# A column-chunk projection whose opening is widened from three chunks to seven, with shift products in column groups

## The reference

```
mod = silu(c) @ w_ada + b_ada                 # 2048 x 6144
shift, scale, gate = split(mod, 3)
h = rms_norm(x, norm_g) * (1 + scale) + shift
proj = h @ w_in                               # 2048 x 13824, parts u, zp, q, kv, za, a, b, zc, gates
y_pool = pooling(u) * silu(zp); y_attn = attention(q, kv) * silu(za)
y_conv = conformer(a * sigmoid(b)) * silu(zc) # depthwise width 31, layer norm, pointwise
merged = sum over branches of sigmoid(gate_i) * (y_i @ w_branch_i)
out = rms_norm(x + gate * (merged @ w_out), final_g)
```

## Time and profile before

| what | value |
|---|---|
| median of three runs | 1021.48 us (1018.66 to 1022.21) |
| profiled execution, time | 1021.49 us |
| profiled execution, span | 1019.7 us |
| TensorE busy | 971.0 us (95%) |
| VectorE busy | 673.6 us (66%) |
| ScalarE busy | 411.3 us (40%) |
| transfers | 220 MB, 216 GB/s on the mean |

### The profile page before, as it was taken

How to read it: one execution, slowest core, us unless ns; L and a number is a source line. 1 busy time by engine, 2 the same in 40 slices (tenths; PEclk the granted TensorE clock), 3 DMA queues, 4 the chain that set the end, 5 groups by cost and what they waited for, 6 DMA issues and landing times.

```text
span 1019.7 us, 10210 instructions
## 1 busy us (share of the span) xinstructions
PE 971.0 (95%) x4227; PEld 755.6 (74%) x4227; DVE 673.6 (66%) x775; ACT 411.3 (40%) x363; POOL 9.8 (1%) x27
## 2 busy tenths in 40 slices
PE   4879999999999999999998999999999999999996
PEld 1124567888888888888887777888888888887885
DVE  3656674767858877876765644368657889766463
ACT  4131244343344334344355434435643333444432
POOL 2000000000000000000000000000000000000000
PEclk9889999999999999999998987999999999999999
DMA  9899997565555565665553343355468998975512
GB/s 313 310 332 366 342 370 240 166 205 166 166 165 187 186 205 179 197 203 184 188 165 124 110 137 125 116 173 199 145 234 315 391 341 300 323 250 182 186 62 82
DMA packets 107758, 220.00 MB, mean 216 GB/s; under 512 B 3665, under 2 KB 3745, under 8 KB 106945
## 3 DMA queue, kind: packets, MB, share of 16 engines
q1 hardware_dynamic: 106304, 212.88, 61.2%
q0 software_dynamic: 1120, 5.43, 1.5%
q10 hardware_dynamic: 288, 1.05, 0.3%
HBM read 217.25 MB, written 2.10 MB: 215 GB/s over the span
## 4 chain that ended last, share of the span: by engine, by line
PE 83%; DVE 6%; DMA 4%; ACT 4%; issue 2%; SPq 0%; DVEq 0%; ACTq 0%
PE acc_odd L941 12%; PE acc_even L941 12%; PE acc_odd L942 12%; PE acc_odd L943 12%; PE acc_even L942 12%; PE acc_even L943 12%; DMA raw<-in_w_ada 4%; PE side_b L969 4%; ACT wh L378 2%; DVE wl L584 2%; DVE ada_sums L631 1%; PE side_a L1052 1%; ACT probs L425 1%; PE side_b L955 1%; PE side_a L955 1%
## 5 line engine op out<-in xcount | busy, mean ns | idle before, releaser
L584 DVE TENSOR_TENSOR wl<-raw,wh 128x2048 fp32r<-128x2048 f32 x152 | 347.7, 2291 | 274.5 <-ACT wh L378 274.2
L378 ACT ACTIVATE wh<-raw 128x2048 fp32r<-128x2048 f32 x152 | 290.7, 1913 | 324.1 <-PE acc_even L943 144.8
L941 PE MATMUL acc_even<-wh,act_h 128*128 128x512 f32 x480 | 192.3, 401 | 1.8 <-DVE glu_a L821 0.9
L941 PE MATMUL acc_odd<-wh,act_h 128*128 128x512 f32 x480 | 189.5, 395 | 1.5 <-DVE wl L584 1.5
L943 PE MATMUL acc_even<-wh,act_l 128*128 128x512 f32 x480 | 188.7, 393 | 0.0
L942 PE MATMUL acc_even<-wl,act_h 128*128 128x512 f32 x480 | 188.5, 393 | 0.0
L943 PE MATMUL acc_odd<-wh,act_l 128*128 128x512 f32 x480 | 187.5, 391 | 0.0
L942 PE MATMUL acc_odd<-wl,act_h 128*128 128x512 f32 x480 | 187.4, 390 | 0.0
L941 PEld LDWEIGHTS acc_even<-wh,act_h 128*128 128x128 f32 x480 | 91.3, 190 | 22.9 <-issue 1.7
L941 PEld LDWEIGHTS acc_odd<-wh,act_h 128*128 128x128 f32 x480 | 90.5, 189 | 23.2 <-issue 2.7
L943 PEld LDWEIGHTS acc_even<-wh,act_l 128*128 128x128 f32 x480 | 91.1, 190 | 19.5
(11 more groups left out here) (239 smaller groups left out, 762.7 us busy)
## 6 DMA issues: line engine op xcount, KB each, us to landing
raw<-in_w_in SPq DMA_DIRECT2D x108, 1024.0 KB, 5.1
raw<-in_w_ada SPq DMA_DIRECT2D x48, 1024.0 KB, 7.0
raw<-in_w_out SPq DMA_DIRECT2D x16, 1024.0 KB, 5.0
raw<-in_w_branch_pool SPq DMA_DIRECT2D x8, 1024.0 KB, 5.0
raw<-in_w_branch_attn SPq DMA_DIRECT2D x8, 1024.0 KB, 4.9
raw<-in_w_branch_conv SPq DMA_DIRECT2D x8, 1024.0 KB, 6.1
raw<-in_conv_pw SPq DMA_DIRECT2D x4, 1024.0 KB, 5.3
x_tok<-in_x SPq DMA_DIRECT2D x1, 2048.0 KB, 8.3
```

The source lines that it names most:

```text
L378: nc.scalar.activation(wh[:, m % RING], raw[:, g % RING], ACT.Copy).then_inc(high_done, 1)
L584: nc.vector.tensor_tensor(wl[:, m % RING], raw[:, load_of(m) % RING], wh[:, m % RING].bitcast(F32), ALU.subtract).then_inc(raw_done, 1)
L941: nc.tensor.matmul(sums[:, h, :], xh, wh[:, slot, i, :], start=begin, stop=False)
```

## The change

Seven chunks are open at once: a0, b0, a1, b1, u0, u1, zp0. Of each K quarter all seven pieces are made before the next quarter: piece m = 7k + j is quarter k of chunk j. The first two chunks stay in the two accumulators. The five others (PARTS) have no room in PSUM: for each token half a quarter's product goes to one of three banks in turn (two of pa, one of pb, `halves`), and is copied to SBUF by ScalarE in quarter 0 (`keep`) or added to it by VectorE in quarters 1 and 2 (`add_part`). The last quarter, pieces 21 to 27, goes through the ordinary loop into accumulators, and VectorE adds the stored sum (`last_part`). ScalarE's evacuations of u0 and u1 go away; sigmoid of b1 and SiLU of zp0 work from SBUF.

The load order has all of the shift and scale loads of quarter k + 1 among the seven weights of quarter k. There are six raw buffers until the load of piece 21, four after.

A shift product has a stationary side of 32 equal columns (c_wide) at column group t for K tile t, so the four products of a shift piece write four different groups of 32 partitions of pb; they are picked and summed over partitions with one more product (`pick`). The scale sums are summed over partitions by products with a column of ones instead of transposes and a reduction. h is made by ScalarE alone (4 ACTIVATEs into h_tmp, one copy to act_h), VectorE makes act_l. VectorE sums scale load 0 before the norm of x. The pool_w load is issued after the transposes of x, no longer after h. Later steps (transposes, pool windows, pool mix, taps) are shifted to new steps; the taps go to steps 26 to 87, four each, instead of 13 to 79.

The loops over k in the diff are, in this order, those of ScalarE, of VectorE and of TensorE; the shift products stand ahead of `halves`.

```diff
+OPEN = ("a0", "b0", "a1", "b1", "u0", "u1", "zp0")
+QUARTERS = 4
+WIDTH = len(OPEN)
+OPENING = WIDTH * QUARTERS
+STAY = 2
+for _i in range(4):
+    LOADS += [("shift", 0, _i), ("scale", 0, _i)]
+for _k in range(QUARTERS):
+    for _j in range(WIDTH):
+        LOADS += [("weights", WIDTH * _k + _j, 0)]
+        if _k + 1 < QUARTERS and 2 <= _j < 6:
+            LOADS += [("shift", _k + 1, _j - 2), ("scale", _k + 1, _j - 2)]
...
+RAWS = 6
...
+    _s = _g % RAWS if _g <= LOAD_OF["weights", WIDTH * (QUARTERS - 1), 0] else min(range(RING), key=_last.get)
...
-TAPS_AT = {m: 4 if m < 22 else 2 if m < 32 else 4 for m in range(13, 80)}
+TAPS_AT = {m: 4 for m in range(26, 88)}
+QUAD = 32
...
+        part_banks = [pa[:, 0:COLS], pa[:, COLS:2 * COLS], pb[:, COLS:2 * COLS]]
+        def part_turn(m, h):
+            return 2 * (PARTS * (m // WIDTH) + m % WIDTH - STAY) + h
...
-            pool.wait_ge(h_ready, 4)
-            pool.wait_ge(consts_ready, 1)
+            pool.wait_ge(x_t, 4)
             pool.dma_start(pool_w[:, :, :, :], a["pool_w"][0].rearrange("g (k p) n -> p g k n", p=P)
                            ).then_inc(pool_w_loaded, 16)
+            pool.wait_ge(h_ready, 4)
...
+            def modulate(q):
+                act.wait_ge(mod_ready, q + 1)
                 if q:
+                    act.wait_ge(h_ready, q)
                 for t in range(PK):
+                    last = nc.scalar.activation(h_tmp[:, t, :], x_chan[:, PK * q + t, :], ACT.Identity,
                                                 scale=mod_scale[:, t:t + 1], bias=mod_shift[:, t:t + 1])
+                last.then_inc(h_full, 1)
+                act.wait_ge(h_full, q + 1)
+                nc.scalar.activation(act_h[:, PK * q:PK * q + PK, :], h_tmp[:, :, :], ACT.Copy).then_inc(h_high, 1)
+            def keep(m):
+                act.wait_ge(used, m + 1)
+                for h in range(TH):
+                    nc.scalar.activation(part[CHUNK_OF[m][0]][:, h, :], part_banks[part_turn(m, h) % 3], ACT.Copy
+                                         ).then_inc(part_copied, 1)
+            for k in range(QUARTERS - 1):
+                m = WIDTH * k
+                split(m + 1)
+                split(m + 2)
+                if k == 1:
+                    keep(m - 1)
+                split(m + 3)
+                split(m + 4)
+                if k == 0:
+                    keep(m + 2)
+                    keep(m + 3)
+                split(m + 5)
+                if k == 0:
+                    keep(m + 4)
+                copy_shift(k + 1)
+                split(m + 6)
+                if k == 0:
+                    keep(m + 5)
+                split(m + 7)
+                modulate(k + 1)
...
+            def last_part(name):
+                total = part[name][:, :, :]
+                dve.wait_ge(used, END[name])
+                dve.wait_ge(part_added, 4 * PARTS)
+                ins = nc.vector.tensor_tensor(total, sums_of(name)[:, :, :], total, ALU.add)
...
+            for k in range(QUARTERS - 1):
+                m = WIDTH * k
+                split(m + 1)
+                split(m + 2)
+                if k == 2:
+                    add_part(m - 1)
+                scale_piece(k + 1, 0)
+                split(m + 3)
+                scale_piece(k + 1, 1)
+                if k:
+                    add_part(m + 2)
+                split(m + 4)
+                scale_piece(k + 1, 2)
+                if k:
+                    add_part(m + 3)
+                split(m + 5)
+                if k:
+                    add_part(m + 4)
+                scale_piece(k + 1, 3)
+                split(m + 6)
+                if k:
+                    add_part(m + 5)
+                modulation_columns(k + 1)
+                split(m + 7)
+                hidden_low(k + 1)
...
                 for t in range(PK):
-                    k = PK * i + t
-                    ins = nc.tensor.matmul(pb[0:1, 0:COLS], c_act[:, k:k + 1], raw[:, g % RING, t, :],
-                                           start=(k == 0), stop=(k == KT - 1))
+                    rows = slice(QUAD * t, QUAD * (t + 1))
+                    ins = nc.tensor.matmul(pb[rows, 0:COLS], c_wide[:, PK * i + t, :], raw[SLOT_OF[g]][:, t, :],
+                                           start=(i == 0), stop=(i == 3), tile_position=(0, QUAD * t))
...
+            def halves(m):
+                pe.wait_ge(raw_done, raws(load_of(m)))
+                for h in range(TH):
+                    turn = part_turn(m, h)
+                    if 3 <= turn < 3 + 2 * PARTS:
+                        pe.wait_ge(part_copied, turn - 2)
+                    elif turn >= 3:
+                        pe.wait_ge(part_added, turn - 2 - 2 * PARTS)
+                    for i in range(PK):
+                        ins = products(act_h, act_l, PK * (m // WIDTH) + i, m % RING, i, part_banks[turn % 3], h,
+                                       i == 0, i == PK - 1)
+                ins.then_inc(used, 1)
...
+            for k in range(QUARTERS - 1):
+                pe.wait_ge(h_ready, k + 1)
+                for j in range(WIDTH):
+                    m = WIDTH * k + j
+                    if j < STAY:
+                        piece(act_h, act_l, PK * k, m, sums_of(OPEN[j]), k == 0, False)
+                    else:
+                        halves(m)
+                    if 1 <= j < 5:
+                        shift_piece(k + 1, j - 1)
+                    if j == 5:
+                        modulation(k + 1)
+            pe.wait_ge(h_ready, QUARTERS)
```

More of the change, by code:

```diff
@@ L68 @@
 LOAD_OF = {load: g for g, load in enumerate(LOADS)}
+RAWS = 6
+SLOT_OF, BEFORE = [], []
+_last = {_s: -1 for _s in range(RAWS)}
+for _g in range(len(LOADS)):
+    _s = _g % RAWS if _g <= LOAD_OF["weights", WIDTH * (QUARTERS - 1), 0] else min(range(RING), key=_last.get)
+    SLOT_OF.append(_s)
+    BEFORE.append(_last[_s])
+    _last[_s] = _g
 def load_of(m):
@@ L75, in landed @@
 def landed(g):
-    return 16 * (g // RING + 1)
+    return 16 * sum(s == SLOT_OF[g] for s in SLOT_OF[:g + 1])
 def shifts(g):
@@ L214, in program @@
         stored = sem("stored")
-        loaded = [sem(f"loaded_{s}") for s in range(RING)]
+        loaded = [sem(f"loaded_{s}") for s in range(RAWS)]
         high_done = sem("high_done")
@@ new lines, in scale_piece @@
+                dve.wait_ge(loaded[SLOT_OF[g]], landed(g))
+                if i:
+                    dve.wait_ge(raw_done, raws(LOAD_OF["scale", q, i - 1]))
+                for t in range(PK):
+                    src, column = raw[SLOT_OF[g]][:, t, :], c_act[:, PK * i + t:PK * i + t + 1]
+                    if i == 0 and t == 0:
+                        last = nc.vector.tensor_scalar(ada_sums[:, :], src, column, None, ALU.mult)
+                    else:
+                        last = nc.vector.scalar_tensor_tensor(ada_sums[:, :], src, column, ada_sums[:, :],
+                                                              ALU.mult, ALU.add)
+                    if t < PK - 1:
+                        chained(last)
@@ new lines, in _ @@
+            dve.wait_ge(var_ready, 1)
+            inverse_root(x_rstd, x_var, newton, 1)
+            for h in range(TH):
+                last = nc.vector.tensor_scalar(x_tok[:, h, :], x_tok[:, h, :], x_rstd[:, h:h + 1], None, ALU.mult)
+            last.then_inc(x_scaled, 1)
+            scale_piece(0, 1)
+            vectors()
+            scale_piece(0, 2)
+            dve.wait_ge(counts_ready, 1)
+            for g in range(4):
+                chained(nc.vector.tensor_scalar(inv_count[:, g, :], inv_count[:, 3, :], float(WINDOWS[g]), None, ALU.min))
@@ L948, in piece @@
                     for h in range(TH):
-                        ins = products(lhs_h, lhs_l, k0, m % RING, i, sums, h, first, last)
+                        ins = products(lhs_h, lhs_l, k0 + i, m % RING, i, sums[:, h, :], h,
+                                       first and i == 0, last and i == PK - 1)
                 ins.then_inc(used, 1)
@@ L1097, in _ @@
                     pe.wait_ge(y_ready, 7 + i)
-                piece(*lhs, PK * i, m, sums_of(name), i == 0, i == pieces - 1)
-                if m == 12:
+                piece(*lhs, PK * i, m, sums_of(name), first, i == pieces - 1)
+                if m == 24:
                     pe.wait_ge(*freed("a0"))
@@ L1193, in _ @@
                     for i in range(PK):
-                        ins = products(act_h, act_l, PK * r, m % RING, i, sums_of("o3"), h, r == 0, r == RING - 1)
+                        ins = products(act_h, act_l, PK * r + i, m % RING, i, sums_of("o3")[:, h, :], h,
+                                       r == 0 and i == 0, r == RING - 1 and i == PK - 1)
                 ins.then_inc(tile_summed, 1)
```

323 lines of the change are left out of this document (141 added, 182 removed).

## The result

The changed kernel takes **983.32 us** (median of 4 runs, 979.65 to 989.05) against 1020.84 us in the same series. The ratio on record is 0.9649, with a 95% interval of 0.9614 to 0.9683; the two medians alone would give 0.9632. Two later series with the same kernel gave 988.49 us and 0.9701 (0.9664 to 0.9737), and 987.34 us and 0.9678 (0.9641 to 0.9714). It is faster by 37.5 us, where the likeliest case had 20 (1001 us). The time is near that of the first rival (988 us).

A forecast was written before the change was run, and what follows sets the result against it. Transfers bound the opening to 141 us, TensorE the rest. Span: 196.1 us to piece 21, 799.0 after it as before, 3.8 more, 998.9 us; forecast 1001 us, own range 994 to 1008, with neighbours 985 to 1017.

The forecast's parts named there:

- the likeliest case: Whole kernel as forecast, a shift piece at 2.3 us: 1001 us, own range 994 to 1008, chance 43%.
- the first rival: Shift products of all four column groups run side by side, 1.15 us a shift piece: 988 us, chance 27%.
- The step that failed: Twelve shift pieces before piece 21: records start in program order, five steps, 2.3 us each, 27.6 us together.
- First product: Opening: the first h quarter is ready and piece 0 can start on TensorE at 44.1 us.
- three modulations: TensorE before piece 21: 16 records of one column each, 1.9 us apiece, 5.7 us together.
- clock: TensorE idles before 44 us and then runs at a lower clock: 2.9 us lost, once.
- quarter ends: Piece j=6 runs while the next h quarter is made; 1.0 us of TensorE waiting in all.
- After piece 21: Rest of the kernel: 799.0 us as before, plus 3.8 us for transposes, the GLU wait and sums on VectorE.
- What hides the rest: Per quarter, transfers (40 or 47 us) and VectorE (36.4 us) stay hidden under TensorE's 49.4 us.
- the slower case: Quarters 1 and 2: VectorE's additions late at the banks, TensorE idles at ten pieces: 1046 us, chance 7%.
- The sum: Forecast's addition of times up to piece 21; pool_w delays scale 3 by 2.7 us to 35.0; total 196.1 us.
- No overlap at all: Fp32 shift products of different column groups never run together, 15 us more: 1016 us, still faster, chance 18%.

The follow-up runs named there:

- the seven executions above: Profiled executions of kernels with four column groups and pool_w issued early, as in the changed kernel; ScalarE begins the split of piece 0 at 36.5 to 39.4 us.

## Why the prediction was right and wrong

**The step that failed** is the one for shift pieces: "If TensorE starts records in program order, the first record of group 1 starts beside the second of group 0, and so on: 5 steps in place of 8". The traces show two steps, all four groups side by side. With 1.20 us for 2.3, twelve shift pieces cost 14.4 and not 27.6 us: 13.2 us, which is most of the miss in the span (998.9 forecast, 983.5 measured). The step of 0.43 us itself was right, though it is not the quotient given for it (3.59/8 is 0.449); it is the distance between starts. My reason, that all records of before start in order, couldn't carry this: they all used the same columns, so nothing could show whether other columns would wait. The first rival, 27%, priced a shift piece at 1.15 us and the time at 988.

That rival was also the one for which the Trainium skill spoke (TensorE: Matmul & The Clock Gate, "Measured speedup vs the span model"): 2.38 times for three column groups. Here four groups give 3.62/1.06 = 3.4 times in the record and 3.72/1.20 = 3.1 on the path, two 1.9 times. Of the drain at a change of tiling mode (TensorEngine Tiling (Array Packing), "Key Properties") nothing is seen: beyond its records a shift piece costs 1.20 - 2 x 0.43 = 0.34 us in groups, and 3.72 - 8 x 0.43 = 0.28 us with one column and no groups.

**The other terms** held. First product at 44.85 us (44.1 forecast), 21 pieces 114.8, three modulations 3 x 1.7 = 5.1 us (5.7), clock 2.7 us (44.85 to 85.10 are 40.25 us for six pieces and four shift pieces that need 37.6; 2.9 forecast, but 1.9 and 1.4 in the two other profiles), quarter ends 0.5 us (1.0). Together 44.85 + 114.8 + 14.4 + 5.1 + 2.7 + 0.5 = 182.35; the timeline shows 182.34. After piece 21: 801.0 us (802.8), with the waits where they were placed, 0.9 for the GLU product, 1.0 and 0.7 for the sums of b1 and u0 on VectorE.

**What hides the rest** was right with its limits. Transfers were hidden, but only by the six buffers (9 to 10 us with four). VectorE's densest step, 6.6 us against 6.7 of TensorE, met it as the first rival said, with 0.16 us to spare, and no bank was late; the slower case did not come, even with 1.4 us more per pair.

**pool_w and the first product.** The sum let pool_w delay scale 3, and with it everything, by 2.7 us. It did not: the sum of scale 3 on VectorE starts at 33.19 us with pool_w early and at 32.93 us with it late, both behind a wait of 0.23 us for the load. In the changed kernel it starts at 34.62 us without a wait, behind VectorE's own work, late in part because the transposes of x ran at the lower clock (1.94 and 1.79 instead of 1.05 us for the first two groups). So the sum's 35.0 us was met for another reason, and that the first product came within 0.8 us of the forecast is in part luck. Piece 0's load does seem to come later by pool_w, but by how much (0.9 to 3.8 us against the seven executions above) one execution doesn't show. In the first profile it cost nothing: h starts at 40.15 us, when the split of piece 0 (40.0) and the modulation (40.1) are both done.

**No overlap at all** was priced at 1016 us; the run with one column gave 1017.7. What the prediction got wrong is a remark there: "Still faster, as the pieces fill time that was idle". At 1016 us this would have been 0.5%; measured 0.2% and not told from nothing. The widening by itself brings next to nothing, because it moves the bound from the transfers to TensorE, whose shift products then cost 45 us in the open.

## What to carry to other kernels

When a stage is bound by one resource and a change hands more work to a second, write down the second's time for the stage before and after: here widening and cheaper shift products each gave about 3 us and together 37, because each half removes the bound that the other leaves. A price that the trace of before can't show, because every instruction there uses the same resource, stays open between its bounds; order seen among instructions that had to be in order is no evidence. And read an edit in the opening from a moment right behind it when the time behind varies by more than the edit is worth.

## What the runs showed of the hardware

- Fp32 products of 128 rows x 32 columns with 512 moving columns, two records of 0.43 us each: four in one column group 3.62 us, in two groups 1.92 us in either order, in four 1.06 us. Records of different groups start together (four within 0.02 us), and the second records start together 0.46 us later. This holds with all groups writing one PSUM bank, in different partitions.
- After 5.2 us of idle the first piece ran at the lower clock for 5.3, 3.6 and 2.7 us in three executions of the changed kernel (a record of 0.77 and then 0.63 us instead of 0.39; granted clock 0.50 from 44.5 to 50 us, which is 1.2 GHz). With unused products in the gap the first record took 0.47 us each time; in two executions the granted clock then was 1.00, in the third it fell from 46.6 to 49.8 us.
- The lower clock also came without idle: behind 16 fp32 records of one column, following full pieces, records took 0.63 us for some 3.3 us in two executions (two groups in turns, one group), which cost 1.6 us each. At the same place nine others show nothing of it.
